# 150 products of the zeroed padding ahead of TensorE's first product, in a streaming encoder step

## What is computed

```python
def trunk_layer(x, ..., lw):
    x = layer_norm(ALPHA * x + 0.5 * swiglu(x, lw['w_ffn1_in'], lw['w_ffn1_out']), g[0], b[0])
    mix, ... = token_mixing(x, ...)   # pooling, latent attention, gated linear attention, gates
    x = layer_norm(ALPHA * x + mix, g[1], b[1])
    x = layer_norm(ALPHA * x + memory_attend(x, mem_k, mem_v, lw['mem_w_q'], lw['mem_w_o']), g[2], b[2])
    x = layer_norm(ALPHA * x + 0.5 * swiglu(x, lw['w_ffn2_in'], lw['w_ffn2_out']), g[3], b[3])
```

## Time and profile before

| What | Value |
|---|---|
| Runs, median of 3 | 2928.51 us (2927.79 to 2928.79) |
| Profiled execution, its own time | 2928.55 us |
| Profiled execution, span from first to last instruction | 2926.8 us |
| Busy: TensorE products, TensorE weight loads | 98%, 94% |
| Busy: VectorE, ScalarE, GpSimd | 36%, 31%, 37% |
| Mean granted TensorE clock | 0.996 |
| Memory read and written | 246.70 MB, 7.87 MB: 87 GB/s |

### The profile page before, as it was taken

One profiled execution on the slowest core, in us unless ns is written; L12 is line 12 of the kernel. 1 busy time (PEld: TensorE's weight loads), 2 busy tenths in 40 slices (PEclk: granted clock), 3 DMA queues, 4 the chain that ended last, 5 costly groups with the idle time before them and its releaser, 6 DMA issues.

```text
span 2926.8 us, 53432 instructions
## 1 busy us (share of the span) xinstructions
PE 2868.9 (98%) x22374; PEld 2764.1 (94%) x22374; DVE 1065.7 (36%) x1871; ACT 914.6 (31%) x1394; POOL 1078.5 (37%) x451
## 2 busy tenths in 40 slices
PE   8999999899999999999999999998999999999997
PEld 8999999699999899999999999986999988999997
DVE  3111245643436562111251111566434364511113
ACT  3222244522334252222242222444223352522222
POOL 3344323134362234333344433331343622333441
PEclk9999999999999999999999999999999999999999
DMA  4222223122252122222222222221222521222221
GB/s 154 86 86 86 88 65 103 33 81 87 94 202 73 44 80 89 88 88 87 83 87 86 86 88 90 85 82 30 89 87 92 205 66 51 80 86 86 86 87 67
DMA packets 75703, 257.04 MB, mean 88 GB/s; under 512 B 10704, under 2 KB 15696, under 8 KB 74256
## 3 DMA queue, kind: packets, MB, share of 16 engines
q1 hardware_dynamic: 67376, 239.55, 25.3%
q10 hardware_dynamic: 8160, 15.05, 1.4%
HBM read 246.70 MB, written 7.87 MB: 87 GB/s over the span
## 4 chain that ended last, share of the span: by engine, by line
PE 87%; DVE 5%; DVEq 4%; issue 2%; ACT 1%; DMA 1%; ACTq 0%; SPq 0%; PEldq 0%
PE PS L352 86%; DVEq L1505 2%; DVE Y L1429 2%; DMA WR<-in_w 1%; PE PS L661 1%; DVEq L1732 0%; ACT LNT L999 0%; DVE XL L1429 0%; DVE O L1432 0%; DVEq L1471 0%; ACTq L1251 0%; DVE SC L1735 0%; PE PS L937 0%; DVE SB L1432 0%; DVE LNT L1432 0%
## 5 line engine op out<-in xcount | busy, mean ns | idle before, releaser
L342 POOL TENSOR_TENSOR WL<-WR,WH 128x1024 fp32r<-128x1024 f32 x445 | 1073.6, 2419 | 1791.3 <-ACT WH L999 1791.2
L352 PE MATMUL PS<-XH,WH 128*128 128x272 f32 x4192 | 918.7, 290 | 19.1 <-DVE WL L1429 12.5
L352 PE MATMUL PS<-XL,WH 128*128 128x272 f32 x4192 | 910.7, 288 | 0.0
L352 PEld LDWEIGHTS PS<-XH,WH 128*128 128x128 f32 x4192 | 674.0, 188 | 31.3 <-issue 15.0
L999 ACT ACTIVATE WH<-WR 128x1024 fp32r<-128x1024 f32 x450 | 474.1, 1056 | 721.4 <-DMA WR<-in_w 714.0
L352 PEld LDWEIGHTS PS<-XL,WH 128*128 128x128 f32 x4192 | 674.8, 189 | 0.0
L352 PE MATMUL PS<-XH,WL 128*128 128x272 f32 x4192 | 648.7, 288 | 0.0
L352 PEld LDWEIGHTS PS<-XH,WL 128*128 128x128 f32 x4192 | 574.5, 188 | 0.0
L1429 DVE TENSOR_TENSOR LNT<-LNT,PS 128x544 f32<-128x544 f32 x88 | 63.5, 721 | 778.3 <-PE PS L352 736.4
L999 ACT ACTIVATE LNT<-PS 128x544 f32<-128x544 f32 (+4 forms) x174 | 102.3, 598 | 726.0 <-PE PS L352 697.7
L352 PE MATMUL PS<-HL,WH 128*128 128x272 f32 x1408 | 299.0, 289 | 0.0
(11 more groups left out here) (230 smaller groups left out, 2859.7 us busy)
## 6 DMA issues: line engine op xcount, KB each, us to landing
WR<-in_w SPq DMA_DIRECT2D x450, 512.0 KB, 3.5
Y<-in_x ACTq DMA_DIRECT2D x4, 544.0 KB, 8.6
MRAW<-in_mem ACTq DMA_DIRECT2D x2, 1024.0 KB, 4.8
MKs<-in_memk_in ACTq DMA_DIRECT2D x2, 1024.0 KB, 6.6
MVs<-in_memv_in ACTq DMA_DIRECT2D x2, 1024.0 KB, 10.0
out_mem_k<-MKp ACTq DMA_DIRECT2D x2, 1024.0 KB, 6.5
out_mem_v<-MVp ACTq DMA_DIRECT2D x2, 1024.0 KB, 8.5
out_y<-Y SPq DMA_DIRECT2D x3, 544.0 KB, 3.0
```

The lines of the kernel that those rows point to most:

```text
L342: pool.tensor_tensor(WL[s][:, :], WR[s][:, :], WH[s][:, :].bitcast(F32), ALU.subtract).then_inc(lo_ready[s], 1)
L352: return pe.matmul(out, lhsT, rhs, start=start, stop=stop, skip_group_check=True)
```

## The change

TensorE waits for a new semaphore, which VectorE raises with the clearing of XH's padding, and then makes 150 products. Each loads the 96 padding columns of XH as weights and streams the same 96 columns, and writes 96 rows x 96 columns of PSUM bank 7, with both the start and the stop flag. They stand behind the five counter increments and ahead of the first layer. The diff, whole:

```diff
--- before.py
+++ after.py
@@ -249,7 +249,7 @@
         lo_ready = [sem(f"w_lo{s}") for s in range(SLOTS)]
         w_used = [sem(f"w_used{s}") for s in range(SLOTS)]
         bank_free = [sem(f"bank_free{b}") for b in range(4)]
-        names = ("const_in small_in x_in0 x_in1 x_in2 x_in3 x_hi x_ready x_done mem_in mem_hi mem_ready mem_st "
+        names = ("pad_ok const_in small_in x_in0 x_in1 x_in2 x_in3 x_hi x_ready x_done mem_in mem_hi mem_ready mem_st "
                  "group_end h_ready y_upd y_sq q_add stats_ready half_mm y_last sq_last st_s st_q st_rd var rstd ln_d y_fin "
                  "hist_in caches_in gla_in pooled pool_mm pool_hi pool_lo kr_ready krp_ok krot_mm "
                  "rq_sq rq_mm rq_v rq_r ck_in latr_hi lat_ready tanh_r gq_ok z_in z_mm z_abs z_l B_ok eb_ok kdE kd_sub kd_ok "
@@ -527,6 +527,11 @@
                     for c in (0, 1):
                         m = mm(PS[:, b + h, 0:TH], ONES, sq[:, c * T + h * TH:c * T + (h + 1) * TH], c == 0, c == 1)
                 return m
+
+
+            pe.wait_ge(S["pad_ok"], 1)
+            for _ in range(150):
+                mm(PS[0:PAD, 7, 0:PAD], XH[:, KC * T:], XH[:, KC * T:], True, True)
 
             for l in range(L):
 
@@ -1515,7 +1520,7 @@
                 if not last:
                     lo(1, KC - 1)
 
-            ve.memset(XH[:, KC * T:].bitcast(F32), 0.0)
+            ve.memset(XH[:, KC * T:].bitcast(F32), 0.0).then_inc(S["pad_ok"], 1)
             ve.memset(XL[:, KC * T:].bitcast(F32), 0.0)
             ve.memset(SC[:, :], 1.0)
             for b in range(4):
```

## The result

The change costs 12.8 us: a median of 2941.34 us (2939.71 to 2943.9, six runs) against 2928.52 us (2927.29 to 2929.51), ratio 1.0043 with a 95% interval of 1.0033 to 1.0053. The forecast was 2928.9 us and the range ended at 2936.1. What happened is close to rival D, to which I had given 0.05.

What follows compares the result with a forecast made beforehand. TensorE, busy 98% of the span, bounds the kernel. The added products push its first real product by 2.05 us and the higher clock saves 1.73, about +0.3 us on 2928.55: 2928.9 us, range 2925.3 to 2936.1.

Steps and rivals of the forecast that it cites:

- rival D: Added products: the clock doesn't rise on them, all 150 go at 0.142 us, +10.1 us, 2938.6 us; chance 0.05.
- what is put ahead of its stream stays in the total: Whole kernel: TensorE is busy 98% of the span, so a microsecond added stays unless TensorE waits there anyway.
- The wait costs nothing by itself: TensorE's start: the wait stands behind the five increments that let the weight loads go, and delays none of them.
- The low stretch of the first real products: First real products, 12.90 to 16.53 us: 17 at 0.227 instead of 0.125 us, 1.73 us to win.
- The load, and not the stream, sets the pace: Added products: the load's pace, 0.076 us high and 0.142 low, was taken over the stream's 0.044 and 0.080.
- 28 products at 0.142 us fill the 3.99 us until the clock rises: Added products: 28 run at the low level, the other 122 take 9.27 us, the last ends at 14.6 us.
- the 3.99 us of before: First real products of the kernel before: TensorE's clock rose after 3.99 us of work.
- the rise at 573 us: Stream at 573 us: the clock rose on plain products of mixed widths, cited against the clock staying low.
- a product of 96 columns at the low level: Added products: three quarters of about 0.10 us gives 0.076 us, times 1.87 gives 0.142 us.
- Rival C: Added products: narrow rounded ones run like plain f32, 0.159 us high and 0.297 low, +12.8 us, 2941.4 us; chance 0.15.
- an earlier TensorE finds its operands for the first 25 us: Beginning: the fourth weight chunk's remainder, ready at 17.6 us, is asked for at 20.2 us, or 18.2 without push.
- one later place of the clock at +-1.6 us: Near 529 us: one fall of the clock more or less costs or saves 1.6 us, taken as 0.

Runs made afterwards that it cites:

- e1_wait_only: The change with its wait and increment kept and the 150 products left out: 2929.46 us against 2928.88 for the kernel before, ratio 1.0001.
- e3_wide: The change with 64 products of zeros, 128 columns loaded and 272 streamed, in place of the 150 narrow ones: 2927.23 us against 2928.88 before, ratio 0.9992.
- e7_wide_then_narrow: The change with 40 wide zero products (128 loaded, 272 streamed), then 60 narrow (96, 96), replacing its 150: 2927.5 us, one execution, beside 2929.49 before.
- e10_wide_again: The kernel with 64 wide products of zeros in place of the change's 150, measured once more: 2925.76 us against 2929.18 before, ratio 0.9989.
- e8_load32_stream96: The change with 200 products of zeros, 32 columns loaded and 96 streamed, in place of its 150: 2925.34 us, one execution, beside 2929.49 before.
- e4_narrow70: The change with 70 of its products in place of 150: 2928.24 us against 2928.88 for the kernel before, ratio 0.9999.
- e2_values: The change with its 150 products made on a scratch tile of three non-zero constants instead of zeroed padding: 2939.28 us against 2928.88 before, ratio 1.0035.

## Why the prediction was wrong

**What held.** TensorE bounds the kernel, and what is put ahead of its stream stays in the total: 13.0 us of push, 12.8 us in the medians. The wait costs nothing by itself (`e1_wait_only`). The low stretch of the first real products is worth 1.8 us at the beginning, near the 1.73 us forecast, where it is really taken away (`e3_wide`: the real products at 0.227 us are gone). The load, and not the stream, sets the pace of a product of 96 by 96.

**The first step that failed** is "28 products at 0.142 us fill the 3.99 us until the clock rises". I took the 3.99 us of before as a property of any work on TensorE. In these runs the rise always came during products whose stream hides their load. The change's products are load-bound, by the very finding on which I had built the pace, and the clock didn't rise on them: 24 us at 1.2 GHz, then a whole low stretch once more. I had this as rival D, and supported its 0.05 with the rise at 573 us; but the products of that stretch stream up to 512 columns, so it was no case of load-bound work. With 0.16 us for each of the 150 the sum gives 24.0 us, and that is the result.

**The second step** is a term that was mis-sized: a product of 96 columns at the low level takes 0.160 us, not 0.142. I had scaled 0.101 us (128 columns, high level) by three quarters and by 1.87. The factor was right (0.160 / 0.085 = 1.88); the base was too low, 0.076 us where `e7_wide_then_narrow` shows 0.085. It came from records of a plain f32 product, and no run shows that those load as fast as rounded ones. The low pace alone makes rival D 2.7 us dearer, 22.6 to 25.3 us for the start of the real products (it was 25.55), and 2938.6 to 2941.3. Had the clock risen after 3.99 us all the same, 25 x 0.160 and 125 x 0.085 us would have ended at 16.0 us, +1.7 us in sum: the forecast would have stood. The first step is the cause. The Trainium skill's price for a load ("TensorE: Matmul & The Clock Gate", section "LDWEIGHTS (loading the stationary operand)"), columns over 1.2 in ns, gives an estimate of 80 ns for 96 columns: near the 0.085 us of the high level, and half of the 0.160 us of the low one.

**Rival C had the right time for the wrong reason**: 2941.4 us from rounded products run like plain f32 ones, 0.159 us each at the high level. The total can't tell the two apart, and my own list of signs gave a pace of 0.16 us to C. What tells them apart is that C had its first 13 products at 0.297 us, while they lie 0.16 us apart from the second on; the real products right behind, 0.227 us apart; and the 0.085 us of `e7_wide_then_narrow`.

**What a gain at the beginning is worth later** was the part that I had only half seen. I checked that an earlier TensorE finds its operands for the first 25 us, and priced one later place of the clock at +-1.6 us. In `e3_wide` the real products are 1.9 us ahead at 30 us, and the last one is 0.3 us later than before (2912.11 instead of 2911.77 us). Most of the gain is lost at 491 us, with the clock at the full level. TensorE comes earlier and waits 1.30 us for GpSimd's remainder of a weight chunk, which is begun no earlier than before (490.09 and 490.12 us). GpSimd, then TensorE:

```profile
490.09 4.72 POOL L342 TENSOR_TENSOR WL<-WR,WH 128x1024 fp32r<-128x1024 f32 x2 [9.68 <-ACT WH L1004]
```

```profile
492.59 0.36 PE L352 MATMUL PS<-QH,WH 128*128 128x272 f32 x1 [1.30 <-POOL WL L342]
```

In the kernel before TensorE doesn't wait there; in `e3_wide` the place costs 1.5 us, in `e10_wide_again`, the same kernel, 0.6 us. The later falls of the clock are the other part. Stretches of TensorE in `e3_wide`:

```profile
531.40:534.80 3.40, 3.40 (x10) 0.50 0.00 0
569.00:575.80 6.80, 6.08 (x18) 0.50 0.00 0
2019.60:2023.10 3.50, 3.50 (x8) 0.51 0.00 0
```

In the twelve profiled executions, the low stretch at 531 us (behind 1.6 to 2.0 us of idle time) is there in seven and missing in five, among them `e8_load32_stream96`; missing, it saves about 1.6 us, so the price I gave that place was right. Those behind the longer idle places, at 569 and at 2020 us, last 3.4 us in some and 6.8 us in others: the longer one costs 1.1 to 1.4 us more at the first place and 0.9 to 1.2 us at the second. These two places weren't in the sum. The two profiled executions of the wide kernel, `e3_wide` and `e10_wide_again`, end 2.6 us apart: 1.6 us from the place at 531 us and 1.0 us from the wait at 491 us. That is more than the whole gain at stake, so the gain has to be read in the timeline of the beginning, not in one total.

**What stays open.** Why the low stretch of the real products is 2.1 us long in `e4_narrow70` and 3.9 to 5.2 us in the others; and which property of a load-bound product keeps the clock low. The runs show only that with a stream of the same width a shorter load changes it, and so does a longer stream over the same load; a load that sets the pace and a stream that pauses for it weren't separated.

## What to carry to other kernels

Check that work meant to raise TensorE's clock is of a kind that raises it. Here products whose stream hides their weight load did (128 or 96 columns loaded and 272 streamed, 32 loaded and 96 streamed), and those with 96 or 128 loaded and 96 streamed didn't. Count filler in time at the level at which it will really run, and let it end before the first real operand is there; in this TensorE-bound kernel every microsecond beyond it was paid in full. A gain of some microseconds at the start is kept only as far as the later operands are ready for it. And look at the spacing of the first real products: it says whether the filler worked.

## What the runs showed of the hardware that was not expected

- 150 load-bound products kept TensorE busy for 24 us without a gap and left it at 1.2 GHz; 200 products with the same stream width and a 32-column load raised it after some 4.7 us.
- 60 load-bound products over 5.1 us didn't lower a clock that was high (`e7_wide_then_narrow`, one execution).
- A product whose rounded load sets the pace takes 0.213 us with 128 columns loaded and 0.160 with 96 at the low level, two cycles of 1.2 GHz for each column; at the high level 96 columns take 0.085 us.
- Zeros or three constants as operands: the same 0.160 us, and no rise in 24 us, either way. Zeros in the wide shape raised the clock after 4.2 and 5.0 us.
- After 1.6 to 2.0 us of idle time near 530 us the clock fell in seven of twelve profiled executions and stayed up in five; two executions of one kernel (`e3_wide`, `e10_wide_again`) differ in it, with idle times of 1.95 and 1.96 us.
- The profile's granted clock reads 1.00 ahead of the first entry in the trace's list of clock changes, also where the products go at the low level (up to 30.77 us in `e2_values`).
